# The first input projection of a two-block transformer kernel: four tiles chunk by chunk instead of two

## The chip, the cores and the metric

One core of a Trainium2 chip. The metric is the device time of one launch in microseconds (us), the median of several runs. Engines are named as in the profile: PE (TensorE) multiplies, DVE (VectorE) and ACT (ScalarE) work elementwise, POOL is GpSimd, SP (SyncE) starts the DMAs.

## The reference

Two transformer blocks in float32 on 512 tokens of width 1024. This is about the very start of the first:

```python
c_act = jax.nn.silu(c)
mod = c_act @ ada_w[l] + ada_b[l]                 # 6 * 1024 columns
sh1, sc1, g1, sh2, sc2, g2 = jnp.split(mod, 6, axis=-1)
h = x * (1.0 + sc1) + sh1
z = h @ w_in                                      # 1024 -> 2816, "in1"
aq, af, ai, ag, bq, bk, bv = split(z)             # gated recurrence and window attention
# f = lb + (1 - lb) * sigmoid(af), k = (1 - lb) * sigmoid(-af), b = cumsum(log f) ...
```

So h needs `sc1` and `sh1`, two of the six parts of the modulation; the other parts are needed later.

## The kernel before, in words

**Layout.** Features lie on partitions. `h` is 8 chunks (`KD`) of 128 features by 512 tokens. The in1 projection has 22 tiles of 128 output features. Each tile sums 8 chunks in one PSUM bank. To keep float32 precision, each operand is split in a high and a low part, and each (tile, chunk) is three matmuls of 512 columns: w_hi h_hi, w_hi h_lo, w_lo h_hi. A weight tile of 512 KB is loaded by SP to `w_raw` (`sp_fetch`, line 308), ACT copies it to `w_hi` (`act_split`, line 318), DVE subtracts for `w_lo` (`dve_split`, line 326). There are two sets of these three buffers, taken in turn. A load waits for the `w_lo` of two tiles before, a `w_hi` for the product of two tiles before. ACT moves a finished tile from PSUM to `z` (`act_keep`, line 384).

**Modulation.** Each 128 columns of `mod` are one job: a load of 512 KB (`sp_job_fetch`, line 457) and one long DVE operation, a product summed along its row (`dve_job`, line 475), called a modulation product here. Those for `sc1` and `sh1` (`START`, 16 jobs, two per chunk of h) have buffers of their own. The next 24 (`IN1`) share two buffers: the load of job j + 2 waits until DVE is done with job j. The buffers lie in what the profile calls `spare`. `_spread` gives each tile slot n of in1 its jobs.

**Order.** Every engine has its instructions in an order written out by hand; each waits on semaphores in that order.
- `sp_start`: inputs, then per chunk f two START loads and the chunk of x; behind chunks 2 and 3 the weight tiles 0 and 1. Weight tile 2 comes at the end.
- `dve_start`: per chunk f its two products, then h_lo of chunk f - 1 (`dve_low`, line 563); behind f = 4 and 5 the splits of tiles 0 and 1.
- `act_start`: per chunk f a modulated copy to `tmp` (line 526), which waits for the second product of the chunk, and the copy to h_hi (line 528); ahead of f = 4 and 5 w_hi of tiles 0 and 1.
- `pe_in1`: tiles 0 and 1 together, chunk by chunk, tile 1 three chunks behind tile 0 (`pe_pair`, line 372), then tiles 2 to 21 one after the other (`pe_product`, line 347), with scores and rotations of the recurrence and of the attention between them.
- `dve_in1`, per slot n: split of tile n + 1; the angle tables (n = 2, 3; lines 728 to 743); gates (n = 4, 5, 7; the large one at lines 1109 to 1114); logarithms and their running sum (n = 9, line 1125); from n = 10 the levels of the recurrence (lines 771, 772, 787, 908), from n = 11 rotations (rope); then the slot's modulation products.

Jobs by slot before: n=0: 0 to 2, n=1: 3 to 5, n=3: 6, n=4: 7, 8, n=5: 9, 10, n=6: 11, 12, n=7: 13, n=8: 14, 15, n=10: 16, n=12: 17, n=14: 18, n=17: 19, n=19: 20, 21, n=20: 22, 23.

Of the kernel before, what the change touches and what calls it, by code (L numbers as in the profile page):

```python
# [111 lines left out]
def in_four(g):  # L112


    return ORDER[g][0] in ("out1", "up00", "down00", "up01", "down01", "up11", "down11")
# [3 lines left out]
    return (1, 3, 0, 2)[g % 4] if in_four(g) else 2 * (g % 2) + bank  # L119


def bank_release(g):
    before = g - 4 if in_four(g) else g - 2
    return (RELEASE[before],) if before >= 0 else ()


# [171 lines left out]

def sp_fetch(k, g):
    if g >= len(ORDER):
        return
    name, n, kt = ORDER[g]
    s, sp = g % 2, k.nc.sync
    if g >= 2:
        sp.wait_ge(*k.seen("w_lo", g - 2))
    sp.dma_start(k.w_raw[s][:, 0:kt * P], k.ins[name][n, :, :]).then_inc(*k.tick(f"w_load{s}", g, 16))


def act_split(k, g):
    if g >= len(ORDER):
        return
    s, w, act = g % 2, ORDER[g][2] * P, k.nc.scalar
    act.wait_ge(*k.seen(f"w_load{s}", g))
    if g >= 2:
        act.wait_ge(*k.seen("product", g - 2))
    act.activation(k.w_hi[s][:, 0:w], k.w_raw[s][:, 0:w], ACT.Copy).then_inc(*k.tick("w_hi", g))  # L318


def dve_split(k, g):
    if g >= len(ORDER):
        return
    s, w, dve = g % 2, ORDER[g][2] * P, k.nc.vector
    dve.wait_ge(*k.seen("w_hi", g))
    dve.tensor_tensor(k.w_lo[s][:, 0:w], k.w_raw[s][:, 0:w], k.w_hi[s][:, 0:w].bitcast(F32), ALU.subtract  # L326
                      ).then_inc(*k.tick("w_lo", g))


# [48 lines left out]

def act_keep(k, g, dst, tokens):
    act, s = k.nc.scalar, g % 2  # L380
    act.wait_ge(*k.seen("product", g))
    for t0, tn, bank in segments(tokens):
        t0 -= TALL - tokens
        last = act.activation(dst[:, t0:t0 + tn], k.ps[:, 2 * s + bank, 0:tn], ACT.Copy)
    last.then_inc(*k.tick("kept", g))


# [36 lines left out]
    return slots  # L424


IN1_SLOTS = _spread(IN1, [3.0, 3.0, 0.5, 0.5, 2.0, 2.0, 2.0, 1.0, 2.0, 0.0] + [0.45] * 7 + [0.3, 0.4, 1.6, 1.6, 0.0])
FFN_SLOTS = _spread(FFN_JOBS, [w for last in (1.6, 1.0) for w in [1.6] * (2 * FG) + [2.7] * KD + [last] * (2 * FG) + [0.8] * KD])


# [64 lines left out]
def sp_start(k):  # L495
    sp, ins = k.nc.sync, k.ins
    sp.dma_start(k.c_act[:, 0, :], ins["c_rows"][:, 0:D].to_broadcast([P, D])).then_inc(*k.tick("c_load", "first", 16))
    sp.dma_start(k.small[:, :], ins["small"]).then_inc(*k.tick("small", None, 16))
    for f in range(KD):
        sp_job_fetch(k, START, 2 * f)  # L500
        sp_job_fetch(k, START, 2 * f + 1)
        sp.dma_start(k.x[:, f, LATS], ins["x"][:, f, :]).then_inc(*k.tick(f"x_load{f}", None, 16))
        if f in (2, 3):
            sp_fetch(k, f - 2)
    sp.dma_start(k.mean[:, :].bitcast(I32), ins["positions"].to_broadcast([P, LAT])).then_inc(*k.tick("consts", "positions", 16))
    sp.dma_start(k.ident[:, :], ins["ident"]).then_inc(*k.tick("consts", None, 16))
# [7 lines left out]
def act_start(k):  # L514
    act = k.nc.scalar
    act.wait_ge(*k.seen("c_load", "first"))
    act.activation(k.c_act[:, 0, :], k.c_act[:, 0, :], ACT.Silu).then_inc(*k.tick("c_act", "first"))
    for f in range(KD):
        h = k.tmp[f % 2][:, :]
        if f in (4, 5):  # L520
            act_split(k, f - 4)
        act.wait_ge(*k.seen(f"x_load{f}"))
        act.wait_ge(*k.seen("mods", START[2 * f + 1].key))
        if f >= 2:
            act.wait_ge(*k.seen("h_lo", ("first", f - 2)))
        act.activation(h, k.x[:, f, LATS], ACT.Identity, scale=k.mod(0, 0, 1, f), bias=k.mod(0, 0, 0, f)).then_inc(*k.tick("first_value", f))
        act.wait_ge(*k.seen("first_value", f))
        act.activation(k.h_hi[:, f, LATS], h, ACT.Copy).then_inc(*k.tick("h_hi", ("first", f)))
    for f in range(KD):
        x = k.x[:, f, LATS]  # L530
        act.activation(x, x, ACT.Copy, scale=ALPHA).then_inc(*k.tick("x_scaled", ("first", f)))


def dve_start(k):
    dve = k.nc.vector
    dve.wait_ge(*k.seen("small"))
    for name in ("ada_b", "mod_b"):
        scales = k.col(name, 0, 2 * NMOD).rearrange("p (l m f) -> p l m f", l=2, m=6)[:, :, 1::3, :]
        last = dve.tensor_scalar(scales, scales, 1.0, None, ALU.add)
    last.then_inc(*k.tick("biases"))  # L540
    dve.wait_ge(*k.seen("biases"))
    dve.wait_ge(*k.seen("c_act", "first"))
    for f in range(KD):
        dve_job(k, START, 2 * f)
        dve_job(k, START, 2 * f + 1)
        if f:
            dve_low(k, "first", f - 1, LATS, k.tmp[(f - 1) % 2][:, :])
        if f in (4, 5):
            dve_split(k, f - 4)
# [19 lines left out]
def sp_in1(k):  # L569
    sp, g0 = k.nc.sync, BASE["in1"]  # L570
    for n in range(IN1_RING):
        sp_job_fetch(k, IN1, n)
    for n in range(22):
        sp_fetch(k, g0 + n + 3)
        if n == 0:
            sp.wait_ge(*k.seen("mods", START[-1].key))
            sp.dma_start(mask_stage(k.hcomb, 1), k.ins["masks1"]).then_inc(*k.tick("load", "masks1", 16))
        for j in IN1_SLOTS[n]:
            sp_job_fetch(k, IN1, j + IN1_RING)
        if n == 5:  # L580
# [19 lines left out]
    return [i for step, i in HG_SCORE_STEPS.items() if HG_TILE + step // KD == n]  # L600


def pe_in1(k):


    g0 = BASE["in1"]
    pe_pair(k, g0, LAT, k.h_hi, k.h_lo, [("h_lo", ("first", c)) for c in range(KD)])
    for n in range(2, 22):
        for c in range(KD):
            pe_product(k, g0 + n, LAT, k.h_hi, k.h_lo, part=range(c, c + 1))  # L610
            step = (n - HG_TILE) * KD + c
# [41 lines left out]
def act_in1(k):  # L653

    g0 = BASE["in1"]
    for n in range(22):
        if n:
            act_split(k, g0 + n + 1)
        if n:
            act_keep(k, g0 + n - 1, k.z1[:, IN1_PLACE[n - 1], :], LAT)  # L660
        if n == 4:
            for i in range(2):
                act_table(k, i)
        if 5 <= n < 9:
            act_hg_gates(k, n - 5)
        if n == 9:
            act_tables(k)
        if n == HG_TILE:
            act_decay(k, "h", 0, hg_combs(k)[0], 1.0)
        for i in hg_levels_beside(n):  # L670
            if i + 1 < LEVELS:
                act_decay(k, "h", i + 1, hg_combs(k)[(i + 1) % 3], 1.0)
        if n == WA_TILE + 8:
            act_v1(k, 0)
        if n == WA_TILE + 10:
            for g in range(2):
# [12 lines left out]
def dve_in1(k):
    g0 = BASE["in1"]  # L690
    for n in range(22):
        if n:
            dve_split(k, g0 + n + 1)
        if n == 2:
            k.nc.vector.wait_ge(*k.seen("consts"))
        if n in (2, 3):
            dve_table(k, n - 2)
        if 4 <= n < 6:
            dve_hg_gates(k, n - 4)
        if n == 7:  # L700
# [2923 lines left out]
```

## Time and profile before

| | us |
|---|---|
| median of 3 runs | 2698.73 (2696.13 to 2701.73) |
| the profiled execution | 2698.6 |
| its span | 2697.3 |
| PE busy in the span | 2551.2 (95%) |
| DVE busy | 1730.9 (64%) |
| ACT busy | 1060.6 (39%) |

Times inside the profile run from the start of the span. A group of instructions is named by line, engine and tiles, out<-in. A busy PE counts a matmul from its start to its modelled end, so that neighbours overlap; from start to start they tell more. "Idle before" names what the engine waited for. The change touches the stage from 0 to about 210 us.

### The profile page before, as it was taken

What the parts mean: (1) busy time and instruction counts of PE and PEld (TensorE: products, weight loads), DVE (VectorE), ACT (ScalarE), POOL (GpSimd) and SP (SyncE); (2) the same over time, 40 slices, a digit from 0 to 9 for tenths busy, and PEclk for the clock granted to TensorE, in tenths of its full rate; (3) what the DMA queues carried; (4) which work ended last, traced back from release to release, by engine and by line L of the source; (5) the groups of instructions that cost most, each with busy time, mean ns of one, the idle gap of its engine ahead of it and who ended that gap; (6) DMA issues with size and microseconds to landing.
All of it is one profiled execution on the core that took longest, in us unless ns stands there. A gap on an engine that the chain in (4) does not pass through costs nothing.

```text
span 2697.3 us, 31833 instructions
## 1 busy us (share of the span) xinstructions
PE 2551.2 (95%) x12988; PEld 2117.6 (79%) x12988; DVE 1730.9 (64%) x2375; ACT 1060.6 (39%) x1452; POOL 24.2 (1%) x31
## 2 busy tenths in 40 slices
PE   4998999999899999898889999999999887999998
PEld 3787788888688888677768888888887676788887
DVE  7886798896798777667434554245534776664563
ACT  4447442232553244432343433133314554442342
POOL 0000000000100000000000000000000000000000
PEclk9999999999899999989999999999999999999999
DMA  8522388663155665111101112111211100223232
GB/s 297 172 95 92 106 295 292 198 197 119 44 172 196 200 209 196 64 40 40 61 9 63 55 63 78 56 63 63 68 58 56 32 24 25 85 96 103 90 103 85
DMA packets 88913, 294.11 MB, mean 109 GB/s; under 512 B 8752, under 2 KB 22704, under 8 KB 88512
## 3 DMA queue, kind: packets, MB, share of 16 engines
q1 hardware_dynamic: 88768, 292.08, 32.3%
q8 instruction: 103, 1.69, 0.3%
q14 instruction: 42, 0.34, 0.0%
HBM read 289.94 MB, written 2.10 MB: 108 GB/s over the span
## 4 chain that ended last, share of the span: by engine, by line
PE 83%; DVE 10%; ACT 4%; issue 2%; DMA 2%; SPq 0%; DVEq 0%; ACTq 0%
PE ps L347 69%; PE ps L372 3%; PE ps L881 2%; PE ps L3053 1%; DVE w_lo L326 1%; DMA spare<-in_ada_w 1%; DVE anm L3304 1%; PE ps L2425 1%; DVE p_lo L3322 1%; PE ps L1886 1%; ACT w_hi L318 1%; DVE h_lo L563 1%; DMA m_start<-in_ada_w 1%; DVE gatt L908 0%; ACT p_hi L3195 0%
## 5 line engine op out<-in xcount | busy, mean ns | idle before, releaser
L347 PE MATMUL ps<-h_hi,w_hi 128*128 128x512 f32 (+1 forms) x2400 | 808.4, 372 | 20.0 <-DVE w_lo L326 19.4
L347 PE MATMUL ps<-h_lo,w_hi 128*128 128x512 f32 (+1 forms) x2400 | 797.6, 368 | 0.0
L347 PE MATMUL ps<-h_hi,w_lo 128*128 128x512 f32 (+1 forms) x2400 | 796.8, 367 | 0.0
L326 DVE TENSOR_TENSOR w_lo<-w_raw,w_hi 128x1024 fp32r<-128x1024 f32 (+2 forms) x319 | 414.2, 1299 | 443.1 <-ACT w_hi L318 441.9
L318 ACT ACTIVATE w_hi<-w_raw 128x1024 fp32r<-128x1024 f32 (+2 forms) x319 | 356.6, 1118 | 757.1 <-PE ps L347 720.8
L347 PEld LDWEIGHTS ps<-h_hi,w_hi 128*128 128x128 f32 x2400 | 451.7, 189 | 105.9 <-DVE w_lo L326 26.3
L347 PEld LDWEIGHTS ps<-h_hi,w_lo 128*128 128x128 f32 x2400 | 453.4, 189 | 76.3
L347 PEld LDWEIGHTS ps<-h_lo,w_hi 128*128 128x128 f32 x2400 | 453.6, 189 | 75.3 <-issue 1.7
L347 PE MATMUL ps<-g_hi,w_hi 128*128 128x512 f32 (+1 forms) x880 | 295.7, 369 | 0.8 <-DVE w_lo L326 0.8
L347 PE MATMUL ps<-g_hi,w_lo 128*128 128x512 f32 (+1 forms) x880 | 294.8, 368 | 0.0
L347 PE MATMUL ps<-g_lo,w_hi 128*128 128x512 f32 (+1 forms) x880 | 294.8, 368 | 0.0
L393 DVE SCALAR_TENSOR_TENSOR x<-ps,mods,x 128x512 f32<-128x512 f32 (+1 forms) x112 | 75.3, 690 | 196.7 <-PE ps L347 187.9
L475 DVE CUSTOM_DVE_ANT_0 m_raw<-m_raw,c_act,small 128x1024 f32<-128x1024 f32 x155 | 196.2, 1281 | 4.4 <-DMA m_raw<-in_ada_w 4.4
L347 PEld LDWEIGHTS ps<-g_hi,w_hi 128*128 128x128 f32 x880 | 165.3, 188 | 29.7 <-DVE w_lo L326 1.4
L347 PEld LDWEIGHTS ps<-g_lo,w_hi 128*128 128x128 f32 x880 | 165.3, 188 | 28.0 <-issue 0.5
L347 PEld LDWEIGHTS ps<-g_hi,w_lo 128*128 128x128 f32 x880 | 165.3, 188 | 27.8
L1822 DVE SCALAR_TENSOR_TENSOR conv_u<-ps,small,conv_u 128x510 f32<-128x510 f32 (+2 forms) x220 | 148.7, 693 | 3.1
L1776 ACT ACTIVATE g_hi<-gated 128x512 fp32r<-128x512 f32 (+1 forms) x88 | 60.5, 687 | 226.9 <-DVE gated L1835 226.9
L1771 ACT ACTIVATE silu_u<-conv_u 128x512 f32<-128x512 f32 (+1 forms) x88 | 60.5, 688 | 203.1 <-DVE conv_u L1822 203.1
L372 PE MATMUL ps<-h_hi,w_hi 128*128 128x256 f32 (+1 forms) x192 | 67.1, 405 | 52.4 <-DVE w_lo L326 27.9
L1837 DVE TENSOR_TENSOR g_lo<-gated,g_hi 128x512 fp32r<-128x512 f32 (+1 forms) x88 | 66.8, 759 | 66.3 <-ACT g_hi L1776 66.3
L372 PEld LDWEIGHTS ps<-h_hi,w_hi 128*128 128x128 f32 x192 | 38.1, 205 | 69.5 <-issue 47.4
(439 smaller groups left out, 2638.5 us busy)
## 6 DMA issues: line engine op xcount, KB each, us to landing
w_raw<-in_up SPq DMA_DIRECT2D x176, 512.0 KB, 3.5
m_raw<-in_w_mod SPq DMA_DIRECT2D x96, 512.0 KB, 3.5
w_raw<-in_down SPq DMA_DIRECT2D x64, 704.0 KB, 4.2
m_raw<-in_ada_w SPq DMA_DIRECT2D x59, 512.0 KB, 4.6
w_raw<-in_in SPq DMA_DIRECT2D x39, 512.0 KB, 3.5
spare<-in_ada_w SPq DMA_DIRECT2D x24, 512.0 KB, 4.2
w_raw<-in_out SPq DMA_DIRECT2D x16, 512.0 KB, 3.4
m_start<-in_ada_w SPq DMA_DIRECT2D x13, 512.0 KB, 11.8
```

What stands on the lines that cost most here:

```text
L318: act.activation(k.w_hi[s][:, 0:w], k.w_raw[s][:, 0:w], ACT.Copy).then_inc(*k.tick("w_hi", g))
L326: dve.tensor_tensor(k.w_lo[s][:, 0:w], k.w_raw[s][:, 0:w], k.w_hi[s][:, 0:w].bitcast(F32), ALU.subtract).then_inc(*k.tick("w_lo", g))
L347: last = pe.matmul(k.ps[:, product_bank(g, bank) if place is None else place, 0:tn], a[:, c, :], b[:, c, t0:t0 + tn], start=c == 0 and n = ...
L372: last = pe.matmul(k.ps[:, product_bank(t, bank), 0:tn], a, b[:, c, t0:t0 + tn], start=c == 0 and n == 0, stop=c == KD - 1 and n == 2)
L393: last = dve.scalar_tensor_tensor(x, k.ps[:, product_bank(g, bank), 0:tn], gates[bank], x, ALU.mult, ALU.add)
L475: dve.tensor_tensor_reduce(w, w, vector, 1.0, bias, ALU.mult, ALU.add, column(last)).then_inc(*k.tick("mods", job.key))
L563: k.nc.vector.tensor_tensor(k.h_lo[:, f, ts], value, k.h_hi[:, f, ts].bitcast(F32), ALU.subtract).then_inc(*k.tick("h_lo", key))
L881: last = pe.matmul(out, unit_of(lhs, rows, cols), right, start=True, stop=True)
L1771: act.activation(f["silu"][:, :], f["conv"][0][:, :], ACT.Silu).then_inc(*k.tick("silu", g))
L1776: act.activation(f["hi"][:, j, :], f["g"][:, :], ACT.Copy).then_inc(*k.tick("g_hi", (block, layer, half, j)))
L1822: last = dve.scalar_tensor_tensor(o, k.ps[:, product_bank(g, bank), lo - d:hi - d], w, o, ALU.mult, ALU.add)
L1837: dve.tensor_tensor(f["lo"][:, j, :], f["g"][:, :], f["hi"][:, j, :].bitcast(F32), ALU.subtract).then_inc(*k.tick("g_lo", key))
```

## The change

Tiles 0 to 3 of in1 are multiplied together, chunk by chunk, in four PSUM banks (`pe_quad` in place of `pe_pair`). Tiles 2 and 3 get weight buffers of their own, laid over memory not yet in use (in them w_lo overwrites w_raw). The loads of the four weight tiles follow START chunks 0 to 3; ACT and DVE split tile f - 2 behind chunk f, for f = 2 to 5. All of x is scaled by ACT only after tiles 0 to 3 have been taken from PSUM. In `dve_in1` and `act_in1` the slots begin at n = 4, both angle tables stand in n = 4, and the jobs are spread anew.

```diff
+FIRST_MORE = (2, 3)
 def bank_release(g):
-    before = g - 4 if in_four(g) else g - 2
+    before = g - 4 if in_four(g) or g in (4, 5) else -1 if g in FIRST_MORE else g - 2
...
+        more = Place(nc, jobs.at + 4 * D)
+        for g in (2, 3):
+            low = Place(nc, more.at)("w_lo%d" % g, [P, D], F32R)
+            self.w_more.append((more("w_raw%d" % g, [P, D]), more("w_hi%d" % g, [P, D], F32R), low))
...
+def tile_before(g):
+    return None if g < 4 else g - 4 if g < 6 else g - 2
...
-IN1_SLOTS = _spread(IN1, [3.0, 3.0, 0.5, 0.5, 2.0, 2.0, 2.0, 1.0, 2.0, 0.0] + [0.45] * 7 + [0.3, 0.4, 1.6, 1.6, 0.0])
+IN1_SLOTS = _spread(IN1, [0.0] * 4 + [0.5, 2.5, 3.0, 1.5, 3.0, 0.5] + [0.75] * 8 + [0.6, 1.8, 1.6, 0.0])
...
 def sp_start(k):
-        if f in (2, 3):
-            sp_fetch(k, f - 2)
+        if f < 4:
+            sp_fetch(k, f)
...
-    sp_fetch(k, 2)
 def act_start(k):
-        if f in (4, 5):
-            act_split(k, f - 4)
         act.wait_ge(*k.seen(f"x_load{f}"))
         act.wait_ge(*k.seen("mods", START[2 * f + 1].key))
...
         act.activation(k.h_hi[:, f, LATS], h, ACT.Copy).then_inc(*k.tick("h_hi", ("first", f)))
+        if 2 <= f < 6:
+            act_split(k, f - 2)
+    for g in range(2):
+        act_split(k, g + 4)
+        act_keep(k, g, k.z1[:, IN1_PLACE[g], :], LAT)
+    for g in FIRST_MORE:
+        act_keep(k, g, k.z1[:, IN1_PLACE[g], :], LAT)
 def dve_start(k):
-        if f in (4, 5):
-            dve_split(k, f - 4)
+        if 2 <= f < 6:
+            dve_split(k, f - 2)
     dve_low(k, "first", KD - 1, LATS, k.tmp[(KD - 1) % 2][:, :])
+    for g in (4, 5):
+        dve_split(k, g)
 def sp_in1(k):
-    for n in range(22):
+    for g in (4, 5):
+        sp_fetch(k, g0 + g)
+    sp.wait_ge(*k.seen("mods", START[-1].key))
+    sp.wait_ge(*k.seen("load", 3))
+    sp.dma_start(mask_stage(k.hcomb, 1), k.ins["masks1"]).then_inc(*k.tick("load", "masks1", 16))
+    for n in range(3, 22):
         sp_fetch(k, g0 + n + 3)
-        if n == 0:
-            sp.wait_ge(*k.seen("mods", START[-1].key))
-            sp.dma_start(mask_stage(k.hcomb, 1), k.ins["masks1"]).then_inc(*k.tick("load", "masks1", 16))
...
+QUAD = [(t, c) for f in range(2, KD + 1) for t, first in ((0, 2), (1, 3), (2, 4), (3, 5)) if f >= first for c in (range(f) if f == first else range(f - 1, f))]
+def pe_quad(k, g):
+    pe, seen = k.nc.tensor, set()
+    for t, c in QUAD:
+        if c == 0:
+            pe.wait_ge(*k.seen("w_lo", g + t))
+        if c not in seen:
+            pe.wait_ge(*k.seen("h_lo", ("first", c)))
+            seen.add(c)
+        _, wh, wl = (w[:, c * P:(c + 1) * P] for w in weights(k, g + t))
+        for n, (a, b) in enumerate(((wh, k.h_hi), (wh, k.h_lo), (wl, k.h_hi))):
+            last = pe.matmul(k.ps[:, (1, 3, 0, 2)[t], 0:LAT], a, b[:, c, LATS], start=c == 0 and n == 0, stop=c == KD - 1 and n == 2)
+        if c == KD - 1:
+            last.then_inc(*k.tick("product", g + t))
 def pe_in1(k):
-    pe_pair(k, g0, LAT, k.h_hi, k.h_lo, [("h_lo", ("first", c)) for c in range(KD)])
-    for n in range(2, 22):
+    pe_quad(k, g0)
+    for n in range(4, 22):
...
 def act_in1(k):
-    for n in range(22):
-        if n:
+    for n in range(4, 22):
+        if n > 4:
             act_split(k, g0 + n + 1)
...
-        if n == 4:
+        if n == 5:
             for i in range(2):
                 act_table(k, i)
...
 def dve_in1(k):
-    for n in range(22):
-        if n:
+    for n in range(4, 22):
+        if n > 4:
             dve_split(k, g0 + n + 1)
-        if n == 2:
+        if n == 4:
             k.nc.vector.wait_ge(*k.seen("consts"))
-        if n in (2, 3):
-            dve_table(k, n - 2)
+            for i in range(2):
+                dve_table(k, i)
```

Jobs by slot after: n=5: 0 to 2, n=6: 3 to 5, n=7: 6, 7, n=8: 8 to 11, n=10: 12, n=11: 13, n=12: 14, n=13: 15, n=15: 16, n=16: 17, n=17: 18, n=18: 19, n=19: 20, 21, n=20: 22, 23.

## Rows read from the trace of the kernel before

**Rows 1.** The page, part 4: share of the ending chain by engine.
```profile
PE 83%; DVE 10%; ACT 4%; issue 2%; DMA 2%; SPq 0%; DVEq 0%; ACTq 0%
```
**Rows 2.** Waits, 0 to 330 us: total us, times, longest us.
```profile
PE ps L372 <- DVE w_lo L326: 27.9, 1, 27.9
...
DVE spare L475 <- DMA spare<-in_ada_w: 13.7, 9, 2.6
...
PE ps L347 <- DVE w_lo L326: 10.4, 8, 4.3
```
**Rows 3.** Stretches: length, then PE, PEld, DVE, ACT, POOL busy, PE clock, DMA.
```profile
48.00:50.00 2.00, 2.00 (x6) 1.52 (x5) 0.92 (x2) 0.00 (x0) 0.00 (x0) 0.50 1.02 305
62.00:128.00 66.00, 60.37 (x287) 48.44 (x286) 58.05 (x76) 36.09 (x35) 1.81 (x1) 1.00 0.51 166
128.00:209.00 81.00, 80.94 (x476) 68.56 (x476) 71.85 (x83) 34.37 (x50) 0.00 (x0) 1.00 0.30 100
43.00:62.00 19.00, 14.27 (x50) 10.62 (x48) 13.34 (x20) 4.49 (x7) 3.49 (x8) 0.82 0.66 213
```
**Rows 4.** The chain in order of time, 23 to 330 us: start, us, what.
```profile
26.03 0.60 DVE h_lo L563
...
39.63 1.20 DVE spare L475
...
56.22 0.35 DVE mean L728
...
66.14 1.20 DVE spare L475
...
67.38 3.87 DMA spare<-in_ada_w
...
78.83 6.03 DMA spare<-in_ada_w
...
87.31 2.21 DVE hk L1109
...
93.05 1.20 DVE spare L475
...
100.71 4.50 DVE hb L1125 x4
...
107.59 1.13 DVE w_lo L326
...
126.91 1.11 DVE w_lo L326
...
128.06 2.33 PE ps L347 x9
...
148.17 5.50 PE ps L347 x24
```
**Rows 5.** Timeline of PE: start, us, instruction, idle before.
```profile
31.42 0.63 PE L372 MATMUL ps<-h_hi,w_lo 128*128 128x512 f32 x1
...
47.70 0.79 PE L347 MATMUL ps<-h_hi,w_hi 128*128 128x512 f32 x1 [4.32 <-DVE w_lo L326]
...
95.45 0.50 PE L347 MATMUL ps<-h_hi,w_hi 128*128 128x512 f32 x1 [2.30 <-DVE w_lo L326]
```
**Rows 6.** Timeline of DVE.
```profile
11.18 1.28 DVE L475 CUSTOM_DVE_ANT_0 m_start<-m_start,c_act,small 128x1024 f32<-128x1024 f32 x1 [0.88 <-DMA m_start<-in_ada_w]
...
14.41 1.28 DVE L475 CUSTOM_DVE_ANT_0 m_start<-m_start,c_act,small 128x1024 f32<-128x1024 f32 x1
...
18.94 1.28 DVE L475 CUSTOM_DVE_ANT_0 m_start<-m_start,c_act,small 128x1024 f32<-128x1024 f32 x1 [1.34 <-DMA m_start<-in_ada_w]
...
68.47 1.22 DVE L1096 TENSOR_SCALAR z<-z 128x2048 f32<-128x2048 f32 x1
```
**Rows 7.** Timeline of ACT in the start.
```profile
21.60 0.81 ACT L526 ACTIVATE tmp<-x,mods 128x512 f32<-128x512 f32 x1 [3.04 <-DVE mods L475]
...
22.98 1.04 ACT L318 ACTIVATE w_hi<-w_raw 128x1024 fp32r<-128x1024 f32 x1
```

More of the change, by code:

```diff
@@ L206, in __init__ @@
         jobs = Place(nc, (nc.sbuf_usable_end - 4 * D * (5 + JOB_RING)) // 64 * 64)
+        more = Place(nc, jobs.at + 4 * D)
         self.c_act = jobs("c_act", [P, 3, D])
+        self.w_more = []
+        for g in (2, 3):
+            low = Place(nc, more.at)("w_lo%d" % g, [P, D], F32R)
+            self.w_more.append((more("w_raw%d" % g, [P, D]), more("w_hi%d" % g, [P, D], F32R), low))
         self.m_term = [jobs(f"m_term{s}", [P, D]) for s in range(2)]
@@ L296, in act_tables, with weights, weights_load @@
     k.nc.scalar.preload_act_table_set("natural_log_exp_and_others")
+def weights(k, g):
+    return k.w_more[g - 2] if g in FIRST_MORE else (k.w_raw[g % 2], k.w_hi[g % 2], k.w_lo[g % 2])
+def weights_load(g):
+    return ({2: "turn_load", 3: "load"}[g] if g in FIRST_MORE else f"w_load{g % 2}"), g
+def tile_before(g):
+    return None if g < 4 else g - 4 if g < 6 else g - 2
 def sp_fetch(k, g):
@@ L304, in sp_fetch @@
     name, n, kt = ORDER[g]
[L305 to L308, printed above, removed]
+    sp = k.nc.sync
+    if tile_before(g) is not None:
+        sp.wait_ge(*k.seen("w_lo", tile_before(g)))
+    sp.dma_start(weights(k, g)[0][:, 0:kt * P], k.ins[name][n, :, :]).then_inc(*k.tick(*weights_load(g), 16))
 def act_split(k, g):
@@ L313, in act_split @@
         return
[L314 to L318, printed above, removed]
+    w, act, (raw, hi, _) = ORDER[g][2] * P, k.nc.scalar, weights(k, g)
+    act.wait_ge(*k.seen(*weights_load(g)))
+    if tile_before(g) is not None:
+        act.wait_ge(*k.seen("product", tile_before(g)))
+    act.activation(hi[:, 0:w], raw[:, 0:w], ACT.Copy).then_inc(*k.tick("w_hi", g))
 def dve_split(k, g):
@@ L323, in dve_split @@
         return
-    s, w, dve = g % 2, ORDER[g][2] * P, k.nc.vector
+    w, dve, (raw, hi, lo) = ORDER[g][2] * P, k.nc.vector, weights(k, g)
     dve.wait_ge(*k.seen("w_hi", g))
-    dve.tensor_tensor(k.w_lo[s][:, 0:w], k.w_raw[s][:, 0:w], k.w_hi[s][:, 0:w].bitcast(F32), ALU.subtract
+    dve.tensor_tensor(lo[:, 0:w], raw[:, 0:w], hi[:, 0:w].bitcast(F32), ALU.subtract
                       ).then_inc(*k.tick("w_lo", g))
@@ L380, in act_keep @@
     act, s = k.nc.scalar, g % 2
+    lower = 1 if g in FIRST_MORE else 0
     act.wait_ge(*k.seen("product", g))
@@ L383, in act_keep @@
         t0 -= TALL - tokens
-        last = act.activation(dst[:, t0:t0 + tn], k.ps[:, 2 * s + bank, 0:tn], ACT.Copy)
+        last = act.activation(dst[:, t0:t0 + tn], k.ps[:, 2 * s + bank - lower, 0:tn], ACT.Copy)
     last.then_inc(*k.tick("kept", g))
@@ L690, in dve_in1 @@
     g0 = BASE["in1"]
-    for n in range(22):
-        if n:
+    for n in range(4, 22):
+        if n > 4:
             dve_split(k, g0 + n + 1)
-        if n == 2:
+        if n == 4:
             k.nc.vector.wait_ge(*k.seen("consts"))
-        if n in (2, 3):
-            dve_table(k, n - 2)
+            for i in range(2):
+                dve_table(k, i)
         if 4 <= n < 6:
```

## The prediction

> **What bounds the kernel now.** I read the chain that ended last first [rows 1]: 83% of it is PE, DVE is 10%. So the change matters only where PE is not fed. The list of waits [rows 2] says where that is in the first 330 us: 27.9 us before the first matmul, and 10.4 us in eight waits for a weight's low part (w_lo, line 326). The stretches [rows 3] place them: from 43 to 62 us PE is busy 14.3 of 19 us at a mean clock of 0.82, from 62 to 128 us it is busy 60.4 of 66, and from 128 to 209 us 80.9 of 81. Hence PE bounds the stage only from 128 us on; until then it waits for w_lo. The chain in order of time [rows 4] says for what: from 39 to 128 us it runs through DVE, its modulation products, splits, tables and gates, and through the DMAs that refill the two buffers of these products (3.87 to 6.03 us each, while DVE stands; 13.7 us in nine waits, rows 2 again). So the number that decides is the time at which DVE has made w_lo of tile 13. Before, it is 126.91 + 1.11 = 128.02, and PE starts that tile at 128.06 [rows 4]. From there PE runs on without a wait, and what tile 13 gains or loses the kernel gains or loses.
>
> **What PE gains by itself.** A tile is 24 matmuls, 5.50 us [rows 4]; three of them, one (tile, chunk), 0.69. Four tiles over the chunks as they come fill PE's gaps, so tile 4 can follow behind chunk 7, where before tiles 2 and 3 are in between, half of one at a clock of 0.5 (1.2 GHz) after a wait of 4.32 us [rows 3, 5]. This is the gain that the edit can bring. Whether it reaches tile 13 depends on DVE.
>
> **The start on DVE, step by step.** Unit prices [rows 4]: a product 1.2 us, h_lo 0.60, w_lo 1.13 and 1.14 with its turn. Before, DVE is done with the last h_lo at 39.6, where the next product starts.
>
> (a) Two more weight tiles (0.52 MB each) go out among the start's loads, and w0 and w1 sooner. Between the data of products 4 and 6 (14.41 and 18.94 in [rows 6]) lie product 5, an x and w0 too, 3.5 tiles' worth, so a tile costs 4.53 / 3.5 = 1.29 us. Product 2, which waited for its data to 11.18, gets it at 12.45; product 4 at 17.0 and product 6 at 21.5, two tiles later each.
>
> (b) Two more splits on DVE before the last chunk: 2 x 1.14 = 2.3 us.
>
> (c) The order of split and chunk. Before, ACT makes w_hi ahead of its wait for the chunk's modulation, so it is there when DVE wants it. After, ACT does it behind tmp and h_hi of the same chunk, and these wait for DVE's second product of that chunk. ACT takes from 21.60 (start of tmp) to 22.98 + 1.04 = 24.02 [rows 7]; with 0.1 to start, DVE sees w_hi 2.55 us after its second product. It has only h_lo (0.60) to do meanwhile, so it stands 1.95 us, in each of four chunks.
>
> So chunk by chunk (second product done; w_lo done). f=2: 17.0 + 2.4 = 19.5; 19.5 + 2.55 + 1.14 = 23.2. From here data are no longer late, and a chunk is 2.42 + 2.55 + 1.14 = 6.1 us: f=3 25.6; 29.3. f=4 31.7; 35.4. f=5 37.8; 41.5. f=6, without a split, 43.9, h_lo to 44.6; f=7 47.0. Its own h_lo needs tmp and h_hi (1.65 us) first and ends at 49.3. **DVE leaves the start at 49.3 against 39.6: 9.7 us late.**
>
> PE meanwhile: the first w_lo is there at 23.2 instead of 27.7, and by my sum PE has caught up when h_lo of chunk 6 comes (47.6). A chunk is then 12 matmuls, 2.7 us. It ends tile 0 at 51.2 and the four at 53.1. ACT makes w_hi of tile 4 behind product 0, 51.2 to 52.35, and w_hi 5 behind product 1; w_lo 4 is done at 53.5, w_lo 5 at 55.05. Tile 4 starts at 53.6. Before, tile 3 was only about to begin then. So the edit does what it says: PE is some 9 us ahead here.
>
> **From 55 us to tile 13, on DVE.** Prices from [rows 4]: both tables 8.8 (56.22 to 66.14 less a split); the large gates 5.75 (87.31 to 93.05); logs 6.9 (100.71 to 107.59); levels 0 and 1 with the first rope 15.85 (107.59 to 126.91 less two splits and a product). The first gate step is 1.2 [rows 6], the four tiny ones I put at 0.75. A product that must wait for its buffer comes 4.0 us after the product two before it (3.87 in the row); 4.9 where a weight tile goes in front, an estimate between the two rows; 6.0 with the table loads around it (as at 78.83). The products' places after: n=5: 0 to 2, n=6: 3 to 5, n=7: 6, 7, n=8: 8 to 11, n=10: 12, n=11: 13.
>
> Tables and first gates: 55.05 + 10.0 = 65.05. n=5: split, tiny gates 66.95, products 0, 1 to 69.35; product 2 waits 2.75, 73.3. n=6: split 74.45, product 3 75.65, product 4 waits 3.65, 80.5, product 5 81.75. n=7: split 82.9, gates 88.65, two products 91.05. n=8: split 92.2; a wait of 1.65; 8, 9 to 96.25; a wait of 3.7; 10, 11 to 102.35. n=9: split 103.5, logs 110.4. n=10: split 111.5, level 0, product 119.65. n=11: split 120.8, rope, level 1, product 130.9. n=12: **w_lo 13 at 132.05 against 128.02, +4.0 us.**
>
> The same as a difference: +9.7 from the start, less two splits already made (2.3), less three products put off behind tile 13 (17 done ahead of it before, 14 after: 3.6), while DVE's idle time is nearly equal (before 13.7 us for data and small rests; after 3.5 for w_hi 4 and 5 and 11.8 for data). About 4 is left. What the edit wins on PE is spent waiting for w_lo again: tiles 7 to 10 start at 74.5, 82.9, 92.2 and 103.5, each 3 to 5 us after PE was ready.
>
> **Bounds.** Refills all at 3.9: 1.8 us less, +2.2. All at 4.9 or more: +5.6. PE itself: tile 10 starts 5 us after tile 9's end, so at half clock. The rows: after 4.32 us of standing PE restarts at 0.5 and that tile takes 2.4 us longer; 2.30 us leave the clock at 1.00 [rows 3, 5]. Three tiles later PE is free at about 132, as late as DVE, so it adds 0.3 at most.
>
> The Trainium skill ("TensorE: Matmul & The Clock Gate", section "HAM oscillation — how this bites in real kernels") says that a matmul loop which waits for its data in every step runs each burst at the low clock, which speaks against this order. By it tiles 7 to 10 each lose 2.4 us; the sum stays, because DVE sets their starts. This trace shows the drop behind 4.32 us and not behind 2.30.
>
> **Behind tile 13.** PE bounds, so the delay stays. DVE carries one product more in each of n=13, 15, 16 and 18 and one less in n=14 and 17; it was busy 71.9 of 81 us there [rows 3] and has room. Product 19 now comes at the end of n=18, so 21's buffer is refilled late: up to 0.6 at the stage's end. I take +0.3. Sum: 4.0 + 0.3 = +4.3 on the profiled execution's 2698.6, that is 2702.9; the median of the runs, 2698.73, is the same time. A difference under 0.2% (5.4 us) is about what a measurement cannot tell from none: 2693.3 to 2704.1.
>
> **Rivals.**
> A, faster. The waits for refills vanish from DVE's path, since its long gates and levels cover them. Then w_lo 13 comes at 132.05 - 11.8 = 120.3; PE, free at about 114, follows: -7.8, 2691. For it: DVE's waits before are refills alone [rows 2]. Against: a ring of two and three or four products in a row, the pattern that made DVE wait nine times. It decides once less than 2 of the 11.8 us are left; with more, it ends in no change. 0.14.
> B, slower. PE has not reached full clock when chunk 6 comes, because the gaps between the chunks keep it low. Twelve matmuls then take 5.1 us instead of 2.7, product 0 ends at 54.0, and w_hi 4 and all of DVE shift by 2.8: 2705.7. For it: the first matmuls before still take 0.63 us each at 31.42, 3.5 us after the first. Against: 2.30 us of standing did not lower it [rows 5]. 0.14.
> C, slower: the products moved to n=13 to 18 use up DVE's room, and PE waits for w_lo or scores behind tile 13, three waits of about 1 us: 2706. 0.12.
> D, no change: DVE's new waits in the start are hidden by late data, and the rest is even: 2698 to 2700. Against: product 6 lands before DVE wants it. 0.10.
>
> **Numbers.** My forecast has 0.50; its own range is 2700.8 to 2705, and a fifth of it lies above 2704.1. Faster by over 0.2%: most of A, 0.13. Slower: B, C and that fifth, with the tails, 0.37. Same: 0.50. Range for 8 in 10: 2692 to 2708.
>
> **What will show it.** Right: DVE's last h_lo of the start near 49; four waits of DVE for w_hi of about 2 us in it; tile 4 near 54; DVE waits of 2 to 4 us for product data between 70 and 100 us; PE waits for w_lo of 3 to 5 us before tiles 7 to 10; tile 13 near 132. Wrong: if DVE leaves the start near 43, step (c) fails; if tile 13 starts before 125, A holds; PE waits behind 135 us mean C.

## The result

The changed kernel is slower: median 2706.06 us over 15 runs (2700.28 to 2714.46) against 2697.53 us of the kernel before in the same sittings. The ratio is 1.0031, 95% interval 1.0019 to 1.0043, so +8.5 us. The forecast of 2702.9 lay 3.2 us under that, but as a difference it was +4.3 us, half of what was measured. The measured time lies outside the sum's own range (2700.8 to 2705) and inside the range of 2692 to 2708; it is one of the cases over 2704.1, which had 0.37.

### The profile after

The stretches of [rows 3], in the changed kernel (the same columns), with two of 2 us that show PE's clock (third column from the end):

```profile
43.00:62.00 19.00, 18.62 (x81) 14.90 (x80) 13.92 (x25) 12.71 (x21) 2.50 (x8) 1.00 0.24 81
62.00:128.00 66.00, 49.88 (x213) 39.60 (x212) 50.82 (x69) 27.80 (x26) 1.81 (x1) 0.87 0.48 163
76.00:78.00 2.00, 2.00 (x6) 1.52 (x6) 0.87 (x3) 1.89 (x1) 0.00 (x0) 0.50 0.98 348
...
104.00:106.00 2.00, 0.00 (x0) 0.00 (x0) 0.53 (x1) 0.00 (x0) 0.00 (x0) 0.50 0.65 199
128.00:209.00 81.00, 81.00 (x471) 68.53 (x472) 74.62 (x90) 37.56 (x52) 0.00 (x0) 1.00 0.36 122
```

From 43 to 62 us PE is now full (18.6 of 19 us, 14.3 before) and its clock stays up. From 62 to 128 us it has lost more than that: 49.9 us busy where it was 60.4, and a clock of 0.87. DVE lost 7 us of work there too. Behind 128 us PE is full in both.

DVE in the start, its timeline (start, us, instruction, idle before), to be read beside [rows 6]:

```profile
12.51 1.28 DVE L498 CUSTOM_DVE_ANT_0 m_start<-m_start,c_act,small 128x1024 f32<-128x1024 f32 x1 [2.18 <-DMA m_start<-in_ada_w]
...
17.03 1.28 DVE L498 CUSTOM_DVE_ANT_0 m_start<-m_start,c_act,small 128x1024 f32<-128x1024 f32 x1 [1.34 <-DMA m_start<-in_ada_w]
...
22.15 1.23 DVE L348 TENSOR_TENSOR w_lo<-w_raw,w_hi 128x1024 fp32r<-128x1024 f32 x1 [1.93 <-ACT w_hi L340]
...
28.32 1.23 DVE L348 TENSOR_TENSOR w_lo<-w_raw,w_hi 128x1024 fp32r<-128x1024 f32 x1 [1.94 <-ACT w_hi L340]
...
34.49 1.23 DVE L348 TENSOR_TENSOR w_lo<-w_raw,w_hi 128x1024 fp32r<-128x1024 f32 x1 [1.94 <-ACT w_hi L340]
...
40.67 1.23 DVE L348 TENSOR_TENSOR w_lo<-w_raw,w_hi 128x1024 fp32r<-128x1024 f32 x1 [1.94 <-ACT w_hi L340]
...
48.93 0.69 DVE L592 TENSOR_TENSOR h_lo<-tmp,h_hi 128x512 fp32r<-128x512 f32 x1 [0.99 <-ACT h_hi L548]
...
54.59 1.23 DVE L348 TENSOR_TENSOR w_lo<-w_raw,w_hi 128x1024 fp32r<-128x1024 f32 x1 [0.20 <-ACT w_hi L340]
```

The four waits for w_hi are there, 1.94 us each and 6.17 us from one to the next. The last h_lo starts at 48.93.

Then PE, the first matmuls of tiles 4 and 7 to 10 and 13 (timeline), as in [rows 5]:

```profile
54.44 0.50 PE L369 MATMUL ps<-h_hi,w_hi 128*128 128x512 f32 x1 [0.38 <-DVE w_lo L348]
...
75.24 0.50 PE L369 MATMUL ps<-h_hi,w_hi 128*128 128x512 f32 x1 [2.50 <-DVE w_lo L348]
...
85.35 0.50 PE L369 MATMUL ps<-h_hi,w_hi 128*128 128x512 f32 x1 [2.77 <-DVE w_lo L348]
...
94.63 0.50 PE L369 MATMUL ps<-h_hi,w_hi 128*128 128x512 f32 x1 [1.91 <-DVE w_lo L348]
...
107.95 0.79 PE L369 MATMUL ps<-h_hi,w_hi 128*128 128x512 f32 x1 [7.59 <-DVE w_lo L348]
...
136.45 0.74 PE L369 MATMUL ps<-h_hi,w_hi 128*128 128x512 f32 x1
```

Tile 4 starts 7.9 us earlier than before (62.30), tile 10 6.9 us later (101.04), tile 13 8.4 us later (128.06). So 14.8 us are lost between tile 4 and tile 10. Of these 11.4 are waits for w_lo (16.1 us against 4.7), and the rest is time at 1.2 GHz inside tiles 7 and 8, which take 7.3 us each instead of 5.5. That rest costs nothing by itself: PE waits again at the end of both, so the time at which DVE has w_lo sets all of it. What DVE waited for in that time, its waits from 70 to 107 us:

```profile
DVE spare L498 <- DMA spare<-in_ada_w: 14.8, 8, 3.6
```

and the refills that the chain in order of time runs through:

```profile
70.05 5.50 DMA spare<-in_ada_w
...
76.89 5.95 DMA spare<-in_ada_w
...
93.47 6.62 DMA spare<-in_ada_w
...
101.43 4.01 DMA spare<-in_ada_w
```

Three of the four, the refills for products 3, 5 and 9, take 5.5 to 6.6 us, where the forecast had at most 4.9, 4.9 and 4.0. The fourth, for product 11, took 4.0, less than the 4.9 of the forecast.

### Where the rest of the kernel goes

The profiled execution of the changed kernel took 2700.28 us, the least of its 15. So it can't be compared as it stands. I lined the traces up at the same matmuls, and ran each kernel once more, unchanged, for a second trace:

> The changed kernel once more, unchanged, for a second trace of it: its profiled execution (2700.28) was the fastest of its 15, 5.8 us under the median, though its first 310 us end 9.0 us later than those of the kernel before. If the clock between 1100 and 1500 us makes the difference (there the profiled execution regained 8 us), this execution keeps the 9 us: about 2706, with PE matmuls at 1.2 GHz in that stretch as in the kernel before. Rival (the change itself speeds up the later stage): it regains them again, about 2700.

> The kernel before once more, unchanged, for a second trace: its first 310 us should repeat to within 1 us, and the differences between its two executions should lie where the granted clock falls.

They took 2704.71 and 2698.79 us. Start of the same matmul against the first trace of the kernel before, in us:

| matmul that before starts at | changed, 1st | changed, 2nd | before, 2nd |
|---|---|---|---|
| 128.06 (tile 13) | +8.4 | +7.5 | -0.8 |
| 308.81 | +9.0 | +6.9 | -1.3 |
| 1100.15 | +9.3 | +6.3 | -2.0 |
| 1500.01 | +1.3 | +6.2 | -2.3 |
| 2690.04 | +1.7 | +6.2 | +0.2 |

The loss arises ahead of tile 13 in both traces. Two traces of one kernel agree to 0.8 and 0.9 us there, and to 1.3 and 2.1 us at 309 us, where I had expected 1 us; so a difference of about 1 us at tile 13 in one trace says nothing. The first one gained 8 us back between 1100 and 1500 us, the second did not. The stretches of PE (length, busy, clock, DMA) from 1100 to 1300 us show why. First trace before, then the two of the changed kernel:

```profile
1100.00:1300.00 200.00, 177.15 (x1082) 0.93 0.13 44
```
```profile
1100.00:1300.00 200.00, 174.79 (x1101) 0.97 0.15 48
```
```profile
1100.00:1300.00 200.00, 177.05 (x1065) 0.93 0.14 45
```

The clock stood at 0.97 once and at 0.93 otherwise. In the instructions, the first trace before has pairs of 256-column matmuls 0.64 us apart at 1128 us (1.2 GHz), the fast trace of the changed kernel 0.35 us at the same place. So the change doesn't speed up that stage. Its price is that of the first stage, 6.9 and 9.0 us, and the median says 8.5.

### The profile page after: what moved, and what is told of

Read it like the earlier page. It is cut to its first block, busy times and chain, and to the rows that moved or that the text cites. A ratio compares the mean times of both kernels' runs of the same rounds, so it can differ in the third digit from the quotient of the medians.

```text
span 2699.0 us, 31830 instructions
## 1 busy us (share of the span) xinstructions
PE 2547.1 (94%) x12988; PEld 2113.4 (78%) x12988; DVE 1729.8 (64%) x2375; ACT 1059.2 (39%) x1452; POOL 23.3 (1%) x31
## 4 chain that ended last, share of the span: by engine, by line
PE 82%; DVE 10%; ACT 4%; issue 2%; DMA 1%; DVEq 0%; ACTq 0%
PE ps L369 69%; PE ps L394 3%; PE ps L930 1%; PE ps L3102 1%; DVE w_lo L348 1%; DMA spare<-in_ada_w 1%; ACT w_hi L340 1%; DVE anm L3353 1%; PE ps L2474 1%; PE ps L1935 1%; DVE p_lo L3371 1%; DVE gatt L957 1%; DVE h_lo L592 0%; DVE spare L498 0%; DVE x L1737 0%
## 5 line engine op out<-in xcount | busy, mean ns | idle before, releaser
L369 PEld LDWEIGHTS ps<-h_hi,w_hi 128*128 128x128 f32 x2384 | 448.4, 189 | 111.8 <-DVE w_lo L348 32.7
L1825 ACT ACTIVATE g_hi<-gated 128x512 fp32r<-128x512 f32 (+1 forms) x88 | 60.4, 686 | 226.7 <-DVE gated L1884 226.7
L1820 ACT ACTIVATE silu_u<-conv_u 128x512 f32<-128x512 f32 (+1 forms) x88 | 60.4, 687 | 202.5 <-DVE conv_u L1871 202.5
L1871 DVE SCALAR_TENSOR_TENSOR conv_v<-ps,small,conv_v 128x511 f32<-128x511 f32 (+1 forms) x132 | 82.9, 656 | 13.5 <-ACT conv_v L1813 12.0
L492 DVE CUSTOM_DVE_ANT_0 m_term<-m_raw,c_act,small 128x1024 f32<-128x1024 f32 x64 | 81.8, 1277 | 0.0
```

What stands on the lines that cost most here:

```text
L369: last = pe.matmul(k.ps[:, product_bank(g, bank) if place is None else place, 0:tn], a[:, c, :], b[:, c, t0:t0 + tn], start=c == 0 and n = ...
L492: dve.tensor_tensor_reduce(k.m_term[n % 2][:, :], w, k.c_act[:, 1, :], 1.0, bias, ALU.mult, ALU.add, column(1)).then_inc(*k.tick("mods", ( ...
L1820: act.activation(f["silu"][:, :], f["conv"][0][:, :], ACT.Silu).then_inc(*k.tick("silu", g))
L1825: act.activation(f["hi"][:, j, :], f["g"][:, :], ACT.Copy).then_inc(*k.tick("g_hi", (block, layer, half, j)))
L1871: last = dve.scalar_tensor_tensor(o, k.ps[:, product_bank(g, bank), lo - d:hi - d], w, o, ALU.mult, ALU.add)
```

## The experiments

Each was timed in 5 rounds against the kernel before. "Tile 13" is the start of its first matmul in the profiled execution; before 128.06, changed 136.45. Experiments 5 to 8 ran on a different chip from the other experiments; their ratios are to the kernel before on that chip.

**1. w_hi ahead of the chunk (in the changed kernel).**

```diff
 def act_start(k):
         h = k.tmp[f % 2][:, :]
+        if 2 <= f < 6:
+            act_split(k, f - 2)
         act.wait_ge(*k.seen(f"x_load{f}"))
...
-        if 2 <= f < 6:
-            act_split(k, f - 2)
```

> The changed kernel with one thing put back: in the start ACT makes w_hi of tile f - 2 ahead of its wait for chunk f, no longer behind it. Theory (DVE sets tile 13, and the four waits of 1.94 us for w_hi are most of its delay): DVE's last h_lo of the start begins near 41.4 instead of 48.9, w_lo of tile 5 ends near 48 instead of 55.7, tile 13 starts about 7.5 us earlier than in the changed kernel, and the median falls by as much, to about 2698.5. Rival (the refills of the product buffers set the pace, so an earlier start only makes DVE wait longer for data): tile 13 moves by less than 2 us. Rival (the loss is PE's clock after its waits): the clock drops stay, the time stays within 2 us of 2706.

Tile 13 at 129.25, 7.2 us earlier than changed. Median 2700.29, ratio 1.0008 (0.9994 to 1.0023). The last h_lo began at 41.44:

```profile
41.44 0.69 DVE L592 TENSOR_TENSOR h_lo<-tmp,h_hi 128x512 fp32r<-128x512 f32 x1 [0.99 <-ACT h_hi L550]
...
46.69 2.65 DVE L348 TENSOR_TENSOR w_lo<-w_raw,w_hi 128x1024 fp32r<-128x1024 f32 x2 [4.56 <-ACT w_hi L340]
```

The start shift of 7.5 us goes through to tile 13. Both rivals fall: the refills don't take it up (DVE's waits for them up to 128 us are 14.0 us here, 14.8 in the changed kernel), and it isn't PE's clock, which still drops (0.83 to 0.86 on average from 68 to 110 us) while the median fell by 5.8 us. With this alone neither a loss nor a gain is left that the interval shows.

**2. Four product buffers (in the changed kernel).** The two new ones lie in the context part of x, empty at that time, for products 0 to 11.

```diff
-        self.m_in1 = [beside_h[:, 4 * i:4 * i + 4, :] for i in range(IN1_RING)]
+        beside_x = self.x[:, :, 0:CTX]
+        self.m_in1 = [a[:, 4 * i:4 * i + 4, :] for a in (beside_h, beside_x) for i in range(2)]
...
+IN1_FOUR = 12
...
+def in1_buffer(n):
+    return n % 4 if n < IN1_FOUR else n % 2
```

> The changed kernel with four buffers instead of two for the modulation products 0 to 11 of IN1 (the two new ones in the part of x that is empty then). The late w_hi of the start stays. Theory (DVE sets tile 13, and its 16.5 us of waits for refills are on the path): the waits fall to 2 or 3 us, tile 13 starts 12 to 15 us earlier than in the changed kernel, about 122 to 125 us, median near 2692. Rival (the start alone is to blame, the refills are hidden): no change, 2706. Rival (PE's clock): the clock drops go with the waits, but tile 13 moves by 5 us at most.

Tile 13 at 122.52, 13.9 us earlier. Median 2692.89, ratio 0.9980 (0.9969 to 0.9992). DVE's waits for product data from 39 to 128 us, 14.8 us in the changed kernel, are

```profile
DVE x L518 <- DMA x<-in_ada_w: 0.3, 1, 0.3
```

So these waits lay on the path, nearly to their full length.

**3. Both.**

> Both edits of the two kernels above in the changed kernel: w_hi ahead and four buffers. Theory: the two add up, since both lie on DVE's path: tile 13 some 20 to 22 us earlier than in the changed kernel, near 115, and the median near 2685, which would be 0.45% under the kernel before. PE alone would allow tile 13 at about 107. If the refills set the pace, the first edit adds nothing to the second.

Tile 13 at 116.98, 19.5 us earlier than changed: 7.2 and 13.9 are 21.1, so they add up but for 1.6. Median 2690.07, ratio 0.9965 (0.9952 to 0.9979). The expected 2685 was not reached: 115 was, nearly, but of the 11.1 us at tile 13 the median keeps 7.6 (over five runs). In this kernel's trace, lined up with that of before, the lead is 11.8 us at 2000 us and 8.5 from 2300 us on, so it is lost far behind this stage; why there is open.

**4. Four buffers in the kernel before** (limit 16 in place of 12).

> The kernel before (two tiles first, old places of the products) with four buffers for the modulation products 0 to 15 of IN1. Theory (before, DVE's 13.7 us of refill waits set PE's pace up to tile 13): PE's waits for w_lo between 43 and 128 us go, tile 13 starts 8 to 11 us earlier, median near 2688. It tells how much of what the version with both edits gains has to do with the four tiles at all: by the theory four tiles then add 3 to 6 us, as PE bounds this one and not that. Rival (DVE's waits before lay beside PE's work): no change from before.

Tile 13 at 120.23, 7.8 us earlier than before; median 2692.22, ratio 0.9977 (0.9966 to 0.9989). That is just under the 8 to 11 us expected, and the median is 4 us over the 2688. The waits for data were on the path before too. PE's waits for w_lo from 39 to 128 us, 9.7 us before, are halved but not gone:

```profile
PE ps L348 <- DVE w_lo L327: 4.7, 3, 2.2
```

Four tiles with both repairs reach tile 13 only 3.3 us earlier than this, and the two medians (2692.22 and 2690.07) have intervals that overlap. The 3.3 us can't be put down to the four tiles alone either. This kernel keeps the old places of the products, 17 of them ahead of w_lo 13, where experiment 3 has 14. What four tiles are worth with the products in equal places was not tried.

**5. The late w_hi in the kernel before.**

```diff
 def act_start(k):
-        if f in (4, 5):
-            act_split(k, f - 4)
         act.wait_ge(*k.seen(f"x_load{f}"))
...
         act.activation(k.h_hi[:, f, LATS], h, ACT.Copy).then_inc(*k.tick("h_hi", ("first", f)))
+        if f in (4, 5):
+            act_split(k, f - 4)
```

> The kernel before (two tiles first) with one thing of the change: ACT makes w_hi of tiles 0 and 1 behind chunks 4 and 5, no longer ahead of them. Theory (in the start nothing hides DVE's wait of 1.95 us for w_hi, and DVE sets tile 13): two waits of 1.95 us, DVE leaves the start 3.9 us later, tile 13 starts near 132 instead of 128.06, median near 2701.5. Rival (DVE's later waits for data take up a late start): tile 13 moves by less than 1.5 us.

DVE's waits from 20 to 40 us:

```profile
DVE w_lo L326 <- ACT w_hi L318: 3.9, 2, 1.9
DVE m_start L475 <- DMA m_start<-in_ada_w: 2.6, 2, 1.3
```

Tile 4 starts 3.6 us later than before, tile 13 2.4 us (130.49); median 2700.32, ratio 1.0017 (1.0003 to 1.0032). The two waits came as expected (before, DVE has no wait for w_hi in this stretch and waits 2.7 us for data). Tile 13 moved by less than the 3.9 us expected: some 1.5 us of it were taken up on the way, as DVE waited 1.4 us less for data from 39 to 128 us (12.3 us, 13.7 before). For that part the rival may hold, but it is hardly more than two traces of one kernel differ by.

**6. Weight loads behind the refills (in the changed kernel, slots 6 to 8).**

```diff
 def sp_in1(k):
     for n in range(3, 22):
-        sp_fetch(k, g0 + n + 3)
+        if not 6 <= n <= 8:
+            sp_fetch(k, g0 + n + 3)
         for j in IN1_SLOTS[n]:
             sp_job_fetch(k, IN1, j + IN1_RING)
+        if 6 <= n <= 8:
+            sp_fetch(k, g0 + n + 3)
```

> The changed kernel in which SP, in slots 6, 7 and 8, starts the weight load behind the slot's refills of product buffers instead of ahead of them. In the changed kernel the refills took 3.9 to 6.6 us, the long ones with a weight load in flight, where the forecast had 4.0 to 6.0. Theory (the weight load takes part of the bandwidth that a refill needs, and this is on DVE's path): the refills behind 76 and 93 us fall from 6.0 and 6.6 to 4 to 5, DVE waits 2 to 4 us less, tile 13 starts 2 to 4 us earlier, median 2702 to 2704. Rival (the refills are long because two of them run at once): refills and time stay.

Tile 13 at 133.73, 2.7 us earlier than changed. Median 2704.15, ratio 1.0028 (1.0017 to 1.0038); this ratio can't tell it from the changed kernel's. The chain's refills in this kernel:

```profile
69.00 3.88 DMA spare<-in_ada_w
...
76.66 4.10 DMA spare<-in_ada_w
...
91.39 5.24 DMA spare<-in_ada_w
...
97.97 4.71 DMA spare<-in_ada_w
```

At 76.7 us it is 4.10 instead of 5.95, at 91.4 5.24 (the weight load is started 0.6 us behind it) instead of 6.62. So a weight load beside them is part of the length of the refills. It is not all, and the rival holds for another part: two refills at once are long without any weight load. The changed kernel's own trace shows it at 70.05, where the refill took 5.50 us. Its SP issues there are

```profile
66.96 0.33 SPq L330 DMA_DIRECT2D w_raw<-in_in  x1
68.84 5.78 SPq L480 DMA_DIRECT2D spare<-in_ada_w  x3
...
75.80 0.43 SPq L330 DMA_DIRECT2D w_raw<-in_in  x1
```

The weight load of 66.96 had landed 3.4 us later, at 70.4, and the next went out behind this refill's end. What ran beside it was the refill of 68.84, until 72.7, and only in its last 1.5 us the next refill and a table load. How much each of the two adds when all run together no run here separates.

**7. Both repairs, and products 0 to 2 in the gap.** In `dve_start`, three products (`IN1_PRE` is 0, 1, 2) stand ahead of the splits of tiles 4 and 5.

```diff
+    for j in IN1_PRE:
+        dve_job(k, IN1, j)
     for g in (4, 5):
         dve_split(k, g)
```

> The version with w_hi ahead and four buffers, with products 0 to 2 put ahead of the splits of tiles 4 and 5, where DVE stood 5.2 us for w_hi of tile 4 (behind product 0 of PE). Theory (DVE's path still sets tile 13 there, 116.98): 3.6 us of DVE's work move into that wait, tile 13 starts near 113.5, median near 2686. Rival (PE bounds that version already): no change, 2690.

Tile 13 at 118.55, 1.6 us later than with the repairs alone (116.98), not 3.5 earlier. Median 2689.20, ratio 0.9970 (0.9959 to 0.9982). The work did move into the gap. Behind the gap DVE now waits elsewhere; its waits in the timeline:

```profile
64.54 1.23 DVE L349 TENSOR_TENSOR w_lo<-w_raw,w_hi 128x1024 fp32r<-128x1024 f32 x1 [1.94 <-ACT w_hi L341]
...
72.91 2.29 DVE L1187 TENSOR_TENSOR hk<-hk,z 128x2048 f32<-128x2048 f32 x1 [2.39 <-ACT z L1112]
...
87.58 1.28 DVE L521 CUSTOM_DVE_ANT_0 x<-x,c_act,small 128x1024 f32<-128x1024 f32 x1 [1.68 <-DMA x<-in_ada_w]
```

ACT makes three steps for the gates (exponential, logarithm, exponential), one per slot, each with a table load of 1.28 us and 1.9 us of work, and DVE's large gates wait for the last of them:

```profile
70.96 1.92 ACT L1112 ACTIVATE z<-z 128x2048 f32<-128x2048 f32 x1
```

Neither theory nor rival had named that. PE waits 2.03 us for w_lo ahead of tile 13, so DVE, not PE, still sets it.

**8. Two buffers, products apart (w_hi ahead).** Pairs: 0, 1 ahead of the splits of tiles 4 and 5; 2, 3 between the tables; 4, 5 behind the first gates; 6 to 11 in slots 5 to 7.

> The changed kernel with w_hi ahead and the old two buffers, its products placed in pairs with some 4 us of other DVE work between the pairs: 0, 1 ahead of the splits of tiles 4 and 5, 2, 3 between the two tables, 4, 5 behind the first gates, 6 to 11 two by two in slots 5 to 7, none in slot 8. Theory (not the number of buffers but three or four products in a row make DVE wait): DVE's waits for data fall from 15.4 us (w_hi ahead alone) to 5 or less, tile 13 starts near 117 to 120, median near 2691, without new memory. Rival (two buffers are too few wherever the products stand): waits stay over 10 us, tile 13 later than 125.

DVE's waits for data from 39 to 128 us, 14.0 us in experiment 1:

```profile
DVE spare L501 <- DMA spare<-in_ada_w: 4.9, 4, 1.8
```

Tile 13 came at 121.64. Median 2691.64, ratio 0.9982 (0.9972 to 0.9992). So some three fifths of what four buffers bring on top of experiment 1 (7.6 of 12.3 us at tile 13) is had by placing the products, without memory. The tile is 1.6 us behind the expected 117 to 120. With the second table pushed back, PE waited 6.33 us ahead of tile 6, and it had no wait at tile 13, so it is PE that is late there.

**9 and 10. Balanced.** Two buffers more, w_hi ahead, products 0 to 2 in the gap, 3, 4 in slot 5, 5 to 7 in slot 6 (ahead of the large gates), 8, 9 and 10, 11 in slots 7 and 8. In the tenth, products 12 and 13 stand behind the split of tile 13 too.

> The version with products 0 to 2 in the gap, whose tile 13 came at 118.55 and not at 113.5: there DVE stood 1.9 us for w_hi and 2.4 us for the gates that ACT makes (ahead of 73 us), and 1.7 us for data at 87. Now products 6 and 7 stand ahead of the large gates, not behind them (slots 5: 3, 4; 6: 5 to 7; 7: 8, 9; 8: 10, 11). Theory (ACT's three gate steps with their table loads, not DVE, set the start of the large gates near 73 us, so only DVE's work behind them counts): the large gates stay near 73, DVE has two products less behind them, tile 13 starts 4 us earlier, near 114.5; median 2685. Rival (DVE's total work counts wherever it stands): no change, 118.5.

> The same, and products 12 and 13 behind the split of tile 13 instead of ahead of it (slots 12: 12; 13: 13; 14: 14; 15: 15, 16; then as before). Theory: DVE's path to tile 13 is 2.4 us shorter, near 112, where PE, free at about 111, bounds; median 2683. Rival (DVE has too little room behind tile 13): PE waits for w_lo or scores between tile 13 and 210 us, and the gain is gone by the stage's end.

The large gates started at 73.64 and 73.04, as expected. Tile 13 came at 117.23 and 115.28. Medians 2685.94 and 2685.84, ratios 0.9955 (0.9938 to 0.9972) and 0.9956 (0.9939 to 0.9974): 10.7 and 10.8 us under the kernel before in the same sitting and the best of the study; both intervals lie clear of 1 and of the changed kernel's. Between the two no difference is shown: the tenth's tile 13 is 2 us earlier, its median is not. The tiles miss their expected 114.5 and 112 by about 3 us. In both, PE's last wait for w_lo is the one ahead of tile 9; in the tenth:

```profile
82.47 0.79 PE L370 MATMUL ps<-h_hi,w_hi 128*128 128x512 f32 x1 [3.76 <-DVE w_lo L349]
```

From there PE bounds, restarting at 1.2 GHz: the stretch from 80 to 85 us has a clock of 0.72, that from 85 to 90 us 0.94 in the tenth and 0.59 in the ninth. I had put PE free at 111; it was free at 115. The restart at 1.2 GHz and the wait of 3.8 us ahead of tile 9 are what I had left out. In both, DVE still waits 2.0 us for ACT ahead of the large gates, so ACT's steps for the gates are the likely next limit; no run tried that.

## Why the forecast was right or wrong

**Right: the place and the sign of each step.** DVE sets the pace up to tile 10, what PE wins by four tiles it gives back waiting for w_lo, and in this stage nothing is regained behind tile 13. The start came out as worked out: products 2 and 4 at 12.51 and 17.03 (12.45 and 17.0), w_lo of tiles 0 to 3 started at 22.15, 28.32, 34.49 and 40.67 (done at 23.2, 29.3, 35.4, 41.5), last h_lo to 49.6 (49.3), tile 4 at 54.44 (53.6). Step (c), the w_hi that ACT makes behind the chunk, is shown by experiment 1, which takes 7.2 us from tile 13. The steps are no shares of the 8.4 us, since experiment 2 takes 13.9 us from the same tile. Experiment 5 shows the step in the kernel before, with two waits.

**Wrong in size: the refills.** "A product that must wait for its buffer comes 4.0 us after the product two before it; 4.9 where a weight tile goes in front." By this DVE's waits for data were 11.8 us, all ahead of w_lo 10, and that was due at 103.5. It came at 107.9, 4.4 us later. Of these 3.0 are the waits, 14.8 us instead of 11.8 (the 16.5 us up to 330 us hold one more, behind tile 13). By pairs of products the waits were 3.1 us (2.75 forecast) for 2 and 3, 4.7 (3.65) for 4 and 5, 4.2 (1.65) for 8 and 9, and 2.8 (3.7) for 10 and 11. So the largest miss is product 9, whose refill took 6.62 us where I had 4.0, and two were priced too high (4.0 us for product 4, not 6.0, and 4.0 for 11, not 4.9). The 4.9 was an estimate between rows of 3.87 and 6.03, with no account of what ran beside each. In the stretches of the three long refills the DMA engines moved 197, 330 and 276 GB/s. The upper bound, "all at 4.9 or more: +5.6", was too low for the same reason. Experiments 2 and 6 and the refill at 70.05 show the term and its causes in part.

**Wrong in size: PE in the start.** 0.7 of the 4.4 us were there at 55.7, when w_lo 5 was done (55.05 forecast). I had PE caught up when h_lo of chunk 6 comes, and tile 0 done at 51.2. PE ran without a pause from 41.95 on and ended tile 0 at 51.98, so ACT began w_hi of tile 4 at 52.07. The last 0.6 us I can't place. The second sum, "the same as a difference", calls DVE's idle time nearly equal, though its own 3.5 + 11.8 is 1.6 us over the 13.7 before; measured it is 4.8 us over (18.5 us).

**Right, but later: who is last at tile 13.** I had DVE at 132.05 and PE "as late as DVE". PE took 28.5 us from tile 10 to tile 13, before 26.3 up to its wait, so 2.2 us for the half clock (2.4 forecast). As tile 10 was later, PE and w_lo 13 (136.3) met again, within 0.2 us, as forecast.

**The clock.** "2.30 us leave the clock at 1.00" holds for the row of before. It is no rule for other waits. PE's stretches in the changed kernel behind its waits of 2.50 us (tile 7, at 75.24), 2.77 us (tile 8, at 85.35) and 1.91 us (tile 9, at 94.63), with the clock third from the end:

```profile
75.00:75.50 0.50, 0.26 (x1) 1.00 0.09 27
75.50:76.00 0.50, 0.50 (x3) 0.94 0.72 223
...
85.00:86.00 1.00, 0.65 (x3) 1.00 0.38 99
86.00:87.00 1.00, 1.00 (x5) 0.59 1.01 309
87.00:88.00 1.00, 1.00 (x4) 0.50 1.07 386
94.60:97.00 2.40, 2.37 (x10) 1.00 0.88 274
```

Tiles 7 and 8 began at 1.00 and fell to 0.50 (76 to 78 us, above) less than 1 us later, while they ran. Tile 9 stayed at 1.00. Tile 10, behind 7.59 us, began at 0.50. The Trainium skill ("TensorE: Matmul & The Clock Gate", section "HAM oscillation — how this bites in real kernels") has a loop that waits for data in every step start each burst at the low clock. The trace agrees at tile 10, in part at tiles 7 and 8, and not at tile 9. Only tile 10's restart was on the path.

**Rivals.** A (refills vanish) is refuted by the 14.8 us of waits ahead of w_lo 10. B (low clock in the start) didn't come: PE's matmuls were 0.23 us apart, full clock, from 29.6 us on, and tile 0 ended at 52.0. C (DVE's room behind tile 13) didn't come either: PE was busy 81.0 of 81 us. D falls with the four waits. The measured time lies where B and C were thought to end, for neither's reason. That the wide range holds it is luck in this sense: the width came from B and C, and the miss from a term whose bound was too low.

## What to carry to other kernels

An instruction moved behind another on its engine inherits that one's waits: w_hi behind the chunk's own copy cost DVE 1.94 us four times, though ACT had time enough ahead of it. Before giving the busiest consumer (here PE) more work early, ask which producer must keep up; here some 14 us lay in DVE waiting for a ring of two buffers, before and after. Doubling the ring without four tiles gained 0.23%, the change as it was made, with four tiles, lost 0.31%, and the four tiles' own share in the best kernels (0.44% under before) is not shown. A refill that is on the path should be priced with everything that runs beside it, not with the median of its kind.

## What the hardware showed that I had not expected

- A refill of 512 KB took 3.9 us at 67.38 in the kernel before, though a weight load started 1.1 us behind it, and 3.9 at 68.84 in the changed kernel. It took 5.5 us when another refill had started 1.2 us ahead and no weight load came, and 6.0 and 6.6 us with a weight load in flight too (for the 6.0, two table loads as well). In the start, with many loads queued, the DMA engines moved 400 GB/s and more.
- PE's clock after standing: waits of 2.50 and 2.77 us were followed by a fall to 0.50 less than 1 us into the next tile, waits of 2.30 and 1.91 us were not.
- Two executions of one kernel can differ by several us far from the change. Two traces of the changed kernel differ by 7.9 us between 1100 and 1500 us, with granted clocks of 0.97 and 0.93 from 1100 to 1300. Another source shows no such clock: experiment 1's profiled execution (2708.14, its median 2700.29) lost 9.6 us between 1500 and 2000 us, with 2832 matmuls where the kernel before has 2887, and both at 1.00. So an execution picked for its trace may be 6 to 8 us off the median.
